# A hybrid attention, S5 and mixture-of-experts layer: lambda computed in the q/k units, routing sums on TensorE, and a router on split parts for four tiles

## The reference, cut to what matters

```python
q, k, v, u = split(rmsnorm(x) @ w_in)             # x: (2048, 1024)
lam = exp(sum(lambda_q1 * lambda_k1)) - exp(sum(lambda_q2 * lambda_k2)) + lam_init
a = softmax(q1 @ k1.T + bias) - lam * softmax(q2 @ k2.T + bias)     # 4 heads, causal
attn = rmsnorm(a @ v, attn_subln) * (1 - lam_init)
x = x + concat([attn, s5_branch(u)]) @ w_out
h = rmsnorm(x, norm_moe)
g_logits = h @ w_router_group + b_router_group    # 4 groups
e_logits = h @ w_router_expert + b_router_expert  # 32 experts, 8 in each group
# top 1 group, top 2 experts in it; two assignments for each token, put in
# expert order with each expert's share padded to blocks of 128 rows
rows = zeros.at[dest].set(h[token])               # dest: block start + rank
out = (silu(rows @ w_gate[e]) * (rows @ w_up[e])) @ w_down[e]       # per block
x = rmsnorm(x + segment_sum(out[dest] * gate, token), norm_final)
```

## Time and profile before

| | |
|---|---|
| Median of 3 runs | 2279.71 us (2276.71 to 2286.16) |
| The profiled execution | 2274.78 us, of which the span 2273.2 us |
| PE, DVE, ACT, POOL busy | 2026.7, 1400.1, 1078.5, 522.9 us |
| q/k units and before; S5; attention | to about 406; to 591; to 1011 us |
| out-projection; routing | 1011 to 1247; 1248 to 1293 us |
| experts; final norm | 1294 to 2210; to 2273 us |

### The profile page before, as it was taken

How to read it: one execution, slowest core, us unless ns; L and a number is a source line. 1 busy time by engine, 2 the same in 40 slices (tenths; PEclk the granted TensorE clock), 3 DMA queues, 4 the chain that set the end, 5 groups by cost and what they waited for, 6 DMA issues and landing times. The chain is left out here.

```text
span 2273.2 us, 32351 instructions
## 1 busy us (share of the span) xinstructions
PE 2026.7 (89%) x10286; PEld 1689.8 (74%) x10287; DVE 1400.1 (62%) x2402; ACT 1078.5 (47%) x1586; POOL 522.9 (23%) x632
## 2 busy tenths in 40 slices
PE   6999999877698989869998399999999999999970
PEld 5888888776587878758887278888888888888860
DVE  4674776457686777754443874585658756455444
ACT  4322211334377777762222264575657656445443
POOL 2000011340000000000000234454445645344340
PEclk9999999898799999989999599999999999999995
DMA  8666977721635233014432497797879978576738
GB/s 263 205 229 215 333 259 228 269 81 57 156 90 121 60 72 74 1 65 134 143 130 102 147 363 247 268 356 228 295 272 372 383 260 302 169 274 203 249 77 311
DMA packets 170682, 458.39 MB, mean 202 GB/s; under 512 B 20496, under 2 KB 69728, under 8 KB 144992
## 3 DMA queue, kind: packets, MB, share of 16 engines
q1 hardware_dynamic: 123616, 285.43, 36.5%
q0 software_dynamic: 30848, 138.24, 19.8%
q10 hardware_dynamic: 16128, 33.56, 4.3%
HBM read 342.08 MB, written 115.10 MB: 201 GB/s over the span
## 5 line engine op out<-in xcount | busy, mean ns | idle before, releaser
L2092 DVE TENSOR_TENSOR w_down_lo<-w_down_raw,w_down_hi 128x2048 fp32r<-128x2048 f32 x64 | 144.0, 2289 | 123.9 <-ACT w_down_hi L2029 123.9
L1318 DVE CUSTOM_DVE_ANT_0 scores<-c_bank,alibi 128x512 f32<-128x512 f32 (+3 forms) x320 | 176.2, 606 | 34.9 <-PE c_bank L1432 34.7
L1458 PE MATMUL c_bank<-v_head,map_T 128*128 128x128 f32 x1088 | 151.8, 285 | 32.3 <-ACT map_T L1372 30.9
L1748 POOL IOTA count_i<- 128x128 int32 x1 | 0.2, 235 | 735.0 <-POOLq L65 735.0
L1458 PEld LDWEIGHTS c_bank<-v_head,map_T 128*128 128x128 f32 x1088 | 135.0, 195 | 44.6 <-ACT map_T L1372 44.0
L2176 PE MATMUL m_bank<-w_down_hi,hidden_T_hi 128*128 128x512 f32 x392 | 159.8, 408 | 6.8 <-DVE w_down_lo L2092 6.8
L2092 DVE TENSOR_TENSOR w_gate_lo<-w_gate_raw,w_gate_hi 128x2048 fp32r<-128x2048 f32 x63 | 141.6, 2289 | 31.2 <-ACT w_gate_hi L2029 30.2
L2155 PE MATMUL m_bank<-w_gate_hi,rows_T_hi 128*128 128x512 f32 x392 | 156.4, 399 | 4.0 <-issue 2.6
L2155 PE MATMUL m_bank<-w_up_hi,rows_T_hi 128*128 128x512 f32 x392 | 159.0, 406 | 0.0
L1363 ACT ACTIVATE scores<-scores,neg_max 128x128 f32<-128x128 f32 (+15 forms) x128 | 153.5, 1199 | 10.6 <-DVE neg_max L1322 10.6
L2156 PE MATMUL m_bank<-w_gate_lo,rows_T_hi 128*128 128x512 f32 x392 | 156.2, 398 | 0.0
(11 more groups left out here) (411 smaller groups left out, 5197.0 us busy)
## 6 DMA issues: line engine op xcount, KB each, us to landing
w_gate_raw<-in_w_gate_dram SPq DMA_DIRECT2D x64, 1024.0 KB, 7.7
w_up_raw<-in_w_up_dram SPq DMA_DIRECT2D x64, 1024.0 KB, 8.1
w_down_raw<-in_w_down_dram POOLq DMA_DIRECT2D x64, 1024.0 KB, 8.1
hT_d<-hT_parts SPq DMA_DIRECT2D x32, 512.0 KB, 4.9
hT_parts<-hT_d SPq DMA_DIRECT2D x32, 512.0 KB, 8.2
k_parts<-kT_d SPq DMA_DIRECT2D x64, 256.0 KB, 7.7
u_tok<-in_x_dram SPq DMA_DIRECT2D x16, 512.0 KB, 6.0
qT_d<-qk_out ACTq DMA_DIRECT2D x32, 256.0 KB, 3.6
```

What stands on the lines that cost most here:

```text
L1318: dve.tensor_tensor_reduce(S[:, s, m, c * BANK:c * BANK + w], bank[2 * (n % 2) + m][:, 0:w], ramp[:, x0:x0 + w], SLOPES[h], -BIG, ALU.add, ...
L1458: last = pe.matmul(bank[6 + u % 2][:, 0:VD], aT[:, n % 2, b * P:(b + 1) * P], v[h % 2][:, kt], start=kt == 0, stop=kt == u % NT)
L2092: dve.tensor_tensor(wlo[w][:, halves[i]], raw[w][:, halves[i]], whi[w][:, halves[i]], ALU.subtract).then_inc(lo_done[w], 1)
```

## The change

Lambda and the scaled gain are made in the q/k units P1 + 28 to P1 + 30; their five loads are issued by GpSimd after the tables of batch 2, and attention's tiles move by 1.5 KiB to make room. The router's weights are split into a high and a low part laid side by side (72 columns); ACT writes the high and DVE the low part of the transposed rows for four tiles, over the space of the unsplit w_out; one group of products gives 72 rows of logits for 512 tokens, and a product with two stacked identities (`two`) adds the parts and turns them back to tokens. The last tile goes alone. The constants of the routing are made by GpSimd during the out-projection. In the routing, `M` is fp32r, PE adds the ones products of all earlier tiles in PSUM, the totals are one reduction, the one-hot matrices are made for eight tiles at a time, and the first gather is issued in the routing stage.

Lambda: the loads and the operations, in `norm_project_prepare` (the same lines leave `attention`'s SyncE and VectorE).

```diff
+    if b == 2:
+        for n, name in enumerate(("lambda_q1", "lambda_k1", "lambda_q2", "lambda_k2")):
+            pool.dma_start(lv[:, n], a[name].to_broadcast([P, HD])).then_inc(lam_in, 16)
+        pool.dma_start(gain_v, a["attn_subln"].rearrange("l (v o) -> (l v) o", o=1)).then_inc(lam_in, 16)
...
+def lambda_at_unit(n):
+    if n == P1 + 28:
+        dve.wait_ge(lam_in, 80)
+        for m in range(2):
+            step(dve.tensor_tensor(lj, lv[:, 2 * m], lv[:, 2 * m + 1], ALU.mult))
+            step(dve.tensor_reduce(ls[:, 0, m:m + 1], lj, AX.X, ALU.add))
+    elif n == P1 + 29:
+        exact_exp(step, dve, ls[:, 1], ls[:, 0], ls[:, 2], ls[:, 3], smi[:, 0:2])
+    elif n == P1 + 30:
+        step(dve.tensor_scalar(ls[:, 4, 0:1], ls[:, 1, 0:1], LAM_INIT, None, ALU.add))
+        step(dve.tensor_tensor(neg_lam, ls[:, 1, 1:2], ls[:, 4, 0:1], ALU.subtract))
+        dve.tensor_scalar(gain_v, gain_v, 1.0 - LAM_INIT, None, ALU.mult).then_inc(gain_v_done, 1)
...
+dve.wait_ge(gain_v_done, 1)
...
-for n, name in enumerate(("lambda_q1", "lambda_k1", "lambda_q2", "lambda_k2")):
-    sp.dma_start(lv[:, n], a[name].to_broadcast([P, HD])).then_inc(lam_in, 16)
-sp.dma_start(gain[:], a["attn_subln"].rearrange("l (v o) -> (l v) o", o=1)).then_inc(lam_in, 16)
...
-    if n == 0:
-        lam()
...
-    act.wait_ge(gain_ready, 1)
```

```diff
+act.wait_ge(wr_in, 64)
+act.activation(wr2[:, :, 0:W], wr[:], ACT.Copy).then_inc(wr2_hi, 1)
+act.wait_ge(wol_done, 4)
...
+def h2_hi(t):
     for h in range(2):
         act.wait_ge(h2T_psum, 2 * t + h + 1)
-        if t and h == 0:
-            act.wait_ge(lg_done, t)
-        act.activation(h2T[:, 4 * h:4 * h + 4], bank[4 + h][:].rearrange("p (k t) -> p k t", k=4), ACT.Copy
-                       ).then_inc(h2T_done, 1)
+        if t and t % GR == 0 and h == 0:
+            act.wait_ge(lgT_done, t // GR)
+        act.activation(hTh[:, 4 * h:4 * h + 4, of(t)], bank[4 + h][:].rearrange("p (k t) -> p k t", k=4), ACT.Copy
+                       ).then_inc(hTh_done, 1)
+def logits_out(g):
+    act.wait_ge(lgT_done, g + 1)
+    if g:
+        act.wait_ge(lg_done, g)
+    cols = slice(0, size(g) * P)
+    act.activation(logits_T[:, cols], bank[6][0:2 * W, cols], ACT.Copy).then_inc(lgT_out, 1)
...
+    if i and i % GR == 0:
+        logits_out(i // GR - 1)
+    if i == NT - 1:
+        logits_out(NT // GR - 1)
+    h2_hi(i)
...
+def h2_lo(t):
+    for h in range(2):
+        dve.wait_ge(hTh_done, 2 * t + h + 1)
+        dve.tensor_tensor(hTl[:, 4 * h:4 * h + 4, of(t)], bank[4 + h][:].rearrange("p (k t) -> p k t", k=4),
+                          hTh[:, 4 * h:4 * h + 4, of(t)], ALU.subtract).then_inc(hTl_done, 1)
+def add_bias(g):
+    dve.wait_ge(lg_done, g + 1)
+    for j in range(size(g)):
+        last = dve.tensor_tensor(logits[:, GR * g + j], bank[7][:, j * W:(j + 1) * W], br[:], ALU.add)
+    last.then_inc(lg_used, 1)
...
+dve.tensor_tensor(two[:], ident[0:2 * W, 0:W], ident[0:2 * W, W:2 * W], ALU.add).then_inc(two_set, 1)
+dve.wait_ge(wr2_hi, 1)
+dve.tensor_tensor(wr2[:, :, W:2 * W], wr[:], wr2[:, :, 0:W], ALU.subtract).then_inc(wr2_lo, 1)
...
+        if i and h == 0:
+            h2_lo(i - 1)
...
+    if i > GR and i % GR == 1:
+        add_bias(i // GR - 1)
+h2_lo(NT - 1)
+add_bias(NT // GR - 1)
+dve.wait_ge(lg_done, NT // GR + 1)
+dve.tensor_tensor(logits[:, NT - 1], bank[0][:, 0:W], br[:], ALU.add).then_inc(last_part, 1)
+dve.wait_ge(last_part, 1)
+dve.tensor_tensor(logits[:, NT - 1], bank[0][:, W:2 * W], logits[:, NT - 1], ALU.add).then_inc(last_part, 1)
...
+def router(g):
+    n = size(g)
+    if g == 0:
+        pe.wait_ge(wr2_hi, 1)
+        pe.wait_ge(wr2_lo, 1)
+    pe.wait_ge(hTh_done, 2 * (GR * g + n))
+    pe.wait_ge(hTl_done, 2 * (GR * g + n))
+    if g:
+        pe.wait_ge(lgT_out, g)
+    o = bank[6][0:2 * W, 0:n * P]
     for k in range(KT):
-        last = pe.matmul(bank[6 + t % 2][:, 0:W], h2T[:, k], wr[:, k], start=k == 0, stop=k == KT - 1)
+        pe.matmul(o, wr2[:, k], hTh[:, k, 0:n * P], start=k == 0, stop=False)
+        last = pe.matmul(o, wr2[:, k], hTl[:, k, 0:n * P], start=False, stop=k == KT - 1)
+    last.then_inc(lgT_done, 1)
+def to_tokens(g):
+    pe.wait_ge(lgT_out, g + 1)
+    if g == 0:
+        pe.wait_ge(two_set, 1)
+    else:
+        pe.wait_ge(lg_used, g)
+    for j in range(size(g)):
+        last = pe.matmul(bank[7][:, j * W:(j + 1) * W], logits_T[:, j * P:(j + 1) * P], two[:], start=True, stop=True)
+    last.then_inc(lg_done, 1)
+def last_router():
+    pe.wait_ge(hTh_done, 2 * NT)
+    for k in range(KT):
+        pe.matmul(bank[0][:, 0:2 * W], hTh[:, k, of(NT - 1)], wr2[:, k], start=k == 0, stop=False)
+    pe.wait_ge(hTl_done, 2 * NT)
+    for k in range(KT):
+        last = pe.matmul(bank[0][:, 0:2 * W], hTl[:, k, of(NT - 1)], wr2[:, k], start=False, stop=k == KT - 1)
     last.then_inc(lg_done, 1)
...
+            if h == 0 and q == 0 and i > GR and i % GR == 1:
+                to_tokens(i // GR - 1)
...
+    if i and i % GR == 0:
+        router(i // GR - 1)
+router(NT // GR - 1)
+to_tokens(NT // GR - 1)
 h2_T(NT - 1)
-router(NT - 1)
+last_router()
```

```diff
+def fill(self, pool, ones):
+    ints = self.count[:].bitcast(I32)
+    pool.iota(ints[:, 0:NT], pattern=[[P, NT]], base=0, channel_multiplier=1).then_inc(self.step, 1)
+    pool.iota(ints[:, NT:NT + 1], pattern=[[1, 1]], base=SEQ, channel_multiplier=1).then_inc(self.step, 1)
+    pool.wait_ge(self.step, 2)
+    pool.tensor_copy(self.tok[:], ints[:, 0:NT]).then_inc(self.step, 1)
+    for k in range(2):
+        pool.tensor_scalar(self.pair[:, k], ints[:, 0:NT], 2.0, float(k + 1), ALU.mult, ALU.add).then_inc(self.step, 1)
+    pool.tensor_scalar(self.spare_pair[:], ints[:, NT:NT + 1], 2.0, 1.0, ALU.mult, ALU.add).then_inc(self.step, 1)
+    pool.wait_ge(self.step, 6)
+    pool.iota(ints, pattern=[[1, P]], base=0, channel_multiplier=0).then_inc(self.step, 1)
+    pool.wait_ge(self.step, 7)
+    pool.tensor_copy(self.count[:], ints).then_inc(self.step, 1)
+    pool.wait_ge(self.step, 8)
+    pool.tensor_scalar(self.thr[:], self.count[:, 0:NT], float(P), None, ALU.mult).then_inc(self.step, 1)
+    pool.affine_select(out=self.earlier[:], in_=ones[:], pattern=[[1, P]], compare_op=ALU.is_gt, fill=0.0,
+                       base=0, channel_multiplier=-1).then_inc(self.step, 1)
+    pool.wait_ge(self.step, 10)
...
-            pe.wait_ge(c_ready, 6)
...
-            dve.wait_ge(c_ready, 6)
```

```diff
-            pe.matmul(bank[0][:], tri[:], m, start=True, stop=True)
-            pe.matmul(bank[1][:], ones[:], m, start=True, stop=True).then_inc(pref_done, 1)
+            pe.matmul(bank[1][:], ones[:].bitcast(F32R), m, start=True, stop=True).then_inc(total_done, 1)
+            pe.matmul(bank[0][:], const.earlier[:], m, start=True, stop=False)
+            for t in range(NT - 1):
+                last = pe.matmul(bank[0][:, (t + 1) * NE:NT * NE].rearrange("p (t e) -> p t e", e=NE), ones[:].bitcast(F32R),
+                                 M[:, t:t + 1].to_broadcast([P, NT - 1 - t, NE]), start=False, stop=t == NT - 2)
+            last.then_inc(pref_done, 1)
...
-                    pe.wait_ge(slots_ready, 2 * (k * NT + i + 1))
+                    if i % 8 == 0:
+                        pe.wait_ge(slots_ready, 2 * (2 * k + i // 8 + 1))
...
-            dve.wait_ge(pref_done, 1)
-            tot = bank[1][:].rearrange("p (t e) -> p t e", e=NE)
-            step(dve.memset(base[:, 0], 0.0))
-            for i in range(NT):
-                step(dve.tensor_tensor(base[:, i + 1], base[:, i], tot[:, i], ALU.add))
+            dve.wait_ge(total_done, 1)
+            step(dve.tensor_reduce(total[:], bank[1][:].rearrange("p (t e) -> p e t", e=NE), AX.X, ALU.add))
...
-            step(dve.tensor_tensor(rank[:], base[:, 0:NT], bank[0][:].rearrange("p (t e) -> p t e", e=NE), ALU.add))
-            step(dve.tensor_tensor(rank[:], rank[:], sbase[:].rearrange("p (o e) -> p o e", o=1).to_broadcast([P, NT, NE]), ALU.add))
+            dve.wait_ge(pref_done, 1)
+            step(dve.tensor_tensor(rank[:], bank[0][:].rearrange("p (t e) -> p t e", e=NE), sbase[:].rearrange("p (o e) -> p o e", o=1).to_broadcast([P, NT, NE]), ALU.add))
...
-                step(dve.tensor_tensor(M[:], Ak[k], rank[:], ALU.mult))
-                step(dve.tensor_reduce(df[:], M[:], AX.X, ALU.add))
+                step(dve.tensor_tensor(at_rank[:], Ak[k], rank[:], ALU.mult))
+                step(dve.tensor_reduce(df[:], at_rank[:], AX.X, ALU.add))
...
-                for i in range(NT):
-                    dve.tensor_scalar(at_row[:, k, i], count[:], place[:, k, 0, i:i + 1], None, ALU.is_equal).then_inc(slots_ready, 1)
-                    dve.tensor_scalar(at_block[:, k, i], count[:, 0:NBLK], place[:, k, 1, i:i + 1], pair[:, k, i:i + 1],
-                                      ALU.is_equal, ALU.mult).then_inc(slots_ready, 1)
+                for h in range(2):
+                    ts = slice(8 * h, 8 * h + 8)
```

(17 more changed lines are left out.)

145 lines of the change are left out of this document (61 added, 84 removed).

## The result

The changed kernel takes 2254.98 us (median of 4 runs, 2249.79 to 2259.93), the kernel before beside it 2281.55 (4 runs). The ratio is 0.9889, with a 95% interval of 0.9864 to 0.9913: 19.8 to 31.0 us faster, 25 in the middle. On another occasion it was 0.9894 (0.9867 to 0.9921; 2253.35 against 2276.53). The forecast was 2250, from 2279.7 and a sum of 29.5 us.

The account below looks back on a forecast made before the run. Bound by PE's in-order tile loop, DVE's routing chain and three waits, with no stage overlap. Terms 3.8 - 0.2 + 11.2 + 1.8 + 1.9 + 4.3 + 2.3 + 4.4 = 29.5 us off median 2279.7: 2250, range 2238 to 2262.

Parts of the forecast that it names:

- Lambda: Attention's start: without lambda's five loads, chunk 1 of q and k comes 3.8 us earlier; bounds 0 and 5.4.
- the rival of covered waits: Chunk 1 no earlier, lambda's packets hold q/k slices, or the clock falls anyway: 4 to 5 us less, 2254; chance 0.17.
- Router in the loop: Out-projection tile loop: three grouped routers replace fourteen per-tile ones, saving 11.2 us; bounds 8.5 and 12.
- The rival of DVE's queue: Tile loop: late low parts delay the norm and PE's transposes; at 7 us late, 9.5 us slower, 2289; chance 0.03.
- Last tile: Last tile's router: PE's gap is filled, so 2.4 GHz holds, saving 1.8 us; bounds -0.3 and 2.2.
- Constants, sums, slots: Routing: savings of 1.9 us (no constants wait), 4.3 (one reduction for 16 additions) and 2.3 (wide slot operations).
- the slots' rival: Routing's slots: by the skill's rule scalar form runs twice tensor form's rate; 6.2 us less gain, 2256; chance 0.05.
- First gather: Gather issued in routing: experts' first product 8.8 us after the ids instead of 13.2, saving 4.4; bounds 1.9 to 6.3.
- the stage changes at 1.6 + 1.1 = 2.7: Routing's end: 1.6 us for copy, hold and issue, then 1.1 for the stage change, counted from the ids.
- Sum: Whole kernel: all terms together save 29.5 us, giving 2245.3 from the profiled execution or 2250 from the median.

Follow-up runs that it names:

- the medians above: Changed kernel timed again, against the changed kernel with lambda and its loads back in attention: 2253.35 and 2255.16 us, 0.9894 and 0.9909 of the kernel before.
- the last column: Attention's first product to the out-projection's, all runs: mean 425.5 us in eight executions with the changed kernel's attention; 427.4 to 428.6 with lambda in attention.
- the fill: Changed kernel plus ten unread 512-column products in PE's gaps around the last tile: last logits 4.23 us after the last transposes start, instead of 5.88.
- its repetition: The changed kernel run once more, unaltered, beside two other kernels: median of 6 runs 2253.35 us, 0.9894 of the kernel before.

## Why the prediction was right, and where it was not

*Lambda.* The transfers came as worked out: unit 4 at 3.1 us instead of 3.8, with PE waiting for the load. The step that failed is the next: the 3.8 us were put into the sum as if attention behind unit 4 ran as before. With PE waiting for chunk 1, the clock was at 1.2 GHz for units 4 and 5, where before it was back at 2.4, and at unit 8 the profiled pair had lost 0.2 us. That is the condition of the rival of covered waits ("the clock falls all the same"), whose 2254 lies nearer to the measured 2254.98 than the forecast's 2250. What the move is worth in all is not settled: 1.8 us by the medians above, with overlapping intervals, 2.5 by the means of the last column (425.5 against 428.0), and perhaps less by the longer S5 stage, which the prediction did not consider.

*Router in the loop.* Right, 11.7 against 11.2: with a group a tile takes 16.39 - 11.79 = 4.60 us more, as forecast, and the subtractions hide in DVE's queue. The rival of DVE's queue did not appear: no transposes wait in the loop.

*Last tile.* Mis-sized: 0.2 instead of 1.8, near the lower bound (-0.3). The choice that the clock holds was wrong, and the fill shows that it was the clock: with it held, 1.5 us more are saved, 1.7 in all.

*Constants, sums, slots.* 1.8, 4.35 and 2.5 against 1.9, 4.3 and 2.3. The first is a wait that went; the other two are counts of DVE operations by their durations in rows of the same shape. One slip of the prediction: the estimate behind the slots' rival (2256) takes 6144 elements for both forms, but the wide form has 4 x (512 + 1024 + 512) = 8192, so by it the edit would look worse still. The sum did not use it.

*First gather.* The failed step is "the stage changes at 1.6 + 1.1 = 2.7". It changed at 6.4, when the rows had landed, so DVE's subtractions were not over at 7.3 but at 10.9, and 3.4 of the 4.4 us were lost: 1.0, below the bound of 1.9. The bound took the issue for the least gain and let nothing new be waited for; but an end of stage is a wait too, and DVE's subtractions were queued behind it.

*Sum.* Three stretches moved for reasons outside the sum: the start (-3.1, the S5 stage), attention behind unit 8 (5.5) and the last stage (-3.9). Without them the profiled pair gained 20.9 us of the 29.5: 1.6 less in the last tile, 3.4 in the gather, 4.0 in attention's start, against 0.5 more in the loop and small terms. The timed ratio, 19.8 to 31.0 us, holds this at its lower end; with the means of attention's last column in place of the one pair it is 23.5. So the forecast fell within its range with 8.6 us of its sum missing in the profiled pair; that the timed gain came out at 25, nearer to 29.5, is in part luck: the other 2 to 4 us are in no stretch that the change explains. The profiled execution before, 4.9 us under its median, was a short one (it has the short S5 stage); taking the median as the base was right.

## What to carry to other kernels

A wait that is removed in front of a transfer can reappear at the transfer, and on PE it can be paid twice, once idle and once at 1.2 GHz behind it; ask what the granted clock of the next units will be before the gain is booked. A gather that GpSimd issues at a stage's end held the stage here until it had landed, so put something useful beside it, but start DVE's long operations on SBUF only when GpSimd has issued. Where a stage is a chain of small operations, counting them by rows of the same shape was right within 0.2 us, for the sums and for the slots.

## What the runs showed of the hardware

- GpSimd's operations of 0.19 us last 2.1 to 2.2 beside a DVE subtraction of 128x2048 from SBUF, and end with it; the issue of an indirect transfer lasts 2.9 instead of 1.0.
- The end of a stage waited for GpSimd's gather: the next stage began 4.3 us after the end of the issue in the changed kernel, and 1.0 and 1.5 us after the landing in two runs that show it; without a gather it began 1.0 us after DVE's last operation.
- PE's clock fell from 2.4 to 1.2 GHz in a stretch with gaps of no more than 0.75 us, between transposes and products of 36 and 72 columns, and held when these gaps were filled.
- In a wait of 2.4 to 2.9 us a clock that was at 2.4 GHz fell to 1.2 in three executions; with 1.9 us of unread products in front of a wait of 2.2 us it held, in one. Through waits of 1.8 (no fill) and 2.0 us (fill) it held too, and fell about 1 us into unit 4.
- The S5 stage, with the same code, took 99.4 to 99.7 us in six executions and 102.7 to 103.4 in eight, and nothing between; the cause was not found.
- The same attention code took 422.8 to 428.5 us. In the windows of 37 us from 630 to 1000 the changed kernel and its repetition have granted clock 1.00 throughout, the kernel before four windows of 0.91 to 0.96; which execution has such dips changed from run to run and was not explained.
